# Even projection of a hybrid recurrent trunk: who asks for the channel-major tokens, and the order of the first pair of units

## What is computed

```python
p = jnp.einsum('bld,de->ble', rmsnorm(h, norm_w), w_in).astype(jnp.float32)
```

## Time and profile before

| what | value |
|---|---|
| median of three runs | 3124.69 us |
| lowest and highest run | 3123.67 and 3127.38 us |
| profiled execution, its own time | 3118.83 us |
| its span | 3117.0 us |
| TensorE (PE) matmul busy | 3001.8 us, 96% |
| PEld / VectorE (DVE) / ScalarE (ACT) / GpSimd (POOL) busy | 87% / 62% / 32% / 16% |
| mean DMA rate over the span | 100 GB/s |

### The profile page before, as it was taken

How to read it: one execution, slowest core, us unless ns; L and a number is a source line. 1 busy time by engine, 2 the same in 40 slices (tenths; PEclk the granted TensorE clock), 3 DMA queues, 4 the chain that set the end, 5 groups by cost and what they waited for, 6 DMA issues and landing times. The chain is left out here.

```text
span 3117.0 us, 89481 instructions
## 1 busy us (share of the span) xinstructions
PE 3001.8 (96%) x38740; PEld 2724.3 (87%) x38740; DVE 1931.6 (62%) x4060; ACT 1001.3 (32%) x2220; POOL 503.9 (16%) x519
## 2 busy tenths in 40 slices
PE   8899999997999999999989999999997999999998
PEld 8899999996888888888779999999995787888886
DVE  4312334445777777777545156776765787888886
ACT  4311210003333443343157122222223344444441
POOL 0000000001333433343310000000001111111112
PEclk9999999998999999999899999999998999999999
DMA  6521212215233333433353221221214223333333
GB/s 219 151 80 66 74 61 76 70 49 167 86 95 119 120 102 119 124 123 101 110 194 115 70 70 63 76 77 60 76 50 156 83 84 90 97 97 97 97 104 129
DMA packets 227704, 311.70 MB, mean 100 GB/s; under 512 B 34792, under 2 KB 166128, under 8 KB 227184
## 3 DMA queue, kind: packets, MB, share of 16 engines
q1 hardware_dynamic: 218160, 276.03, 27.7%
q0 software_dynamic: 9152, 29.94, 3.2%
HBM read 210.18 MB, written 95.72 MB: 98 GB/s over the span
## 5 line engine op out<-in xcount | busy, mean ns | idle before, releaser
L410 DVE SCALAR_TENSOR_TENSOR po_stage<-po_work,po_cw,po_stage 128x424 f32<-128x424 f32 (+1 forms) x360 | 232.1, 645 | 28.3 <-issue 1.7
L588 PE MATMUL po_ps<-po_xnT_hi,po_w_hi 128*128 128x424 f32 x960 | 205.0, 355 | 0.0
L588 PE MATMUL po_ps<-po_xnT_hi,po_w_lo 128*128 128x424 f32 x960 | 204.4, 355 | 0.0
L588 PE MATMUL po_ps<-po_xnT_lo,po_w_hi 128*128 128x424 f32 x960 | 204.1, 354 | 0.0
L302 ACT ACTIVATE po_work<-po_ps 128x424 f32<-128x424 f32 (+1 forms) x120 | 61.6, 514 | 408.1 <-PE po_ps L588 408.1
L588 PEld LDWEIGHTS po_ps<-po_xnT_hi,po_w_hi 128*128 128x128 f32 x960 | 180.3, 188 | 5.2
L588 PEld LDWEIGHTS po_ps<-po_xnT_hi,po_w_lo 128*128 128x128 f32 x960 | 180.4, 188 | 4.5
L588 PEld LDWEIGHTS po_ps<-po_xnT_lo,po_w_hi 128*128 128x128 f32 x960 | 180.2, 188 | 4.6
L588 PE MATMUL pe_ps<-pe_w_hi,pe_xnT_hi 128*128 128x256 f32 x1088 | 154.4, 285 | 19.3 <-ACT pe_xnT_hi L302 15.4
L588 PEld LDWEIGHTS pe_ps<-pe_w_hi,pe_xnT_hi 128*128 128x128 f32 x1088 | 140.7, 193 | 21.5 <-issue 17.3
L588 PE MATMUL pe_ps<-pe_w_lo,pe_xnT_hi 128*128 128x256 f32 x1088 | 153.5, 284 | 0.0
(11 more groups left out here) (463 smaller groups left out, 7138.6 us busy)
## 6 DMA issues: line engine op xcount, KB each, us to landing
me_ring<-scratch_w_lo SPq DMA_DIRECT2D x68, 512.0 KB, 3.8
mo_c<-scratch_ch_o SPq DMA_DIRECT2D x51, 512.0 KB, 3.6
scratch_ch_o<-po_stage SPq DMA_DIRECT2D x96, 212.0 KB, 1.9
scratch_tok_e<-pe_stage SPq DMA_DIRECT2D x136, 128.0 KB, 1.9
pe_raw<-in_w_in_e POOLq DMA_DIRECT2D x52, 256.0 KB, 4.2
me_xs<-scratch_ch_e SPq DMA_DIRECT2D x17, 768.0 KB, 6.4
po_raw<-in_w_in_o POOLq DMA_DIRECT2D x48, 256.0 KB, 3.8
scratch_ch_e<-pe_stage SPq DMA_DIRECT2D x52, 212.0 KB, 1.9
```

The source lines that it names most:

```text
L410: return nc.vector.scalar_tensor_tensor(out=o, in0=a, scalar=s, in1=b, op0=op0, op1=op1)
L588: last = nc.tensor.matmul(out, left.bitcast(F32R), right.bitcast(F32R), start=(i == 0 and k == 0), stop=(i == 2 and k == KD - 1))
```

## The change

Four things, all in the even projection:

- `products()`: in the first pair the second unit lags by two tiles. The list is now (0, 0), (0, 1), (0, 2), (1, 0), (0, 3), (1, 1), ... (0, 16), (1, 14), (1, 15), (1, 16).
- The requests for tile t+2, channel-major and token-major, move from SyncE's queue to ScalarE's: the first stands ahead of the rounding of tile t+1, the second behind the root of tile t. In the prologue the channel-major tile 1 is asked for ahead of both token-major tiles.
- ScalarE takes the root of tile t behind the rounding of tile t+1 (before: of t+1), and rounds unit 1's weights behind the first root.
- VectorE takes the rest of tile t+1, then the reciprocal of tile t (before: of t+1), then scales tile t+2; unit 1's weights are split behind the first reciprocal, ahead of the scaling of tile 2.

```diff
@@ def products()
-            for t in range(NT):
+            lag = 2 if late else 0
+            for t in range(NT + lag):
                 for u in range(EARLY):
-                    yield u, ("tok", t)
+                    if 0 <= t - u * lag < NT:
+                        yield u, ("tok", t - u * lag)
@@ @block.sync
+            if late:
+                load_xt(1)
             for t in range(0 if late else 1, XB):
                 load_x(t)
-                if late and t:
-                    load_xt(t)
...
-                if u == 0 and what[1] + XB < NT:
-                    if late:
-                        sp.wait_ge(s_xs, what[1] + 1)
-                        load_xt(what[1] + XB)
-                        sp.wait_ge(s_rt, what[1] + 1)
-                    else:
-                        sp.wait_ge(s_tr, what[1] + 1)
+                if u == 0 and what[1] + XB < NT and not late:
+                    sp.wait_ge(s_tr, what[1] + 1)
                     load_x(what[1] + XB)
@@ @block.scalar
             if late:
                 round_x(0)
                 round_weights(0)
-                root(0)
...
-            round_weights(1)
+                round_weights(1)
             for n, (u, what) in ORDER:
+                if late and u == 0 and what[1] + XB < NT:
+                    act.wait_ge(s_xs, what[1] + 1)
+                    act.dma_start(xT[what[1] % XB], x_in[:, what[1] + XB]).then_inc(s_xt[what[1] % XB], 16)
                 if u == 0 and what[1] + 1 < NT:
                     round_x(what[1] + 1)
-                    if late:
-                        root(what[1] + 1)
-                    elif what[1] + 2 < NT:
+                    if not late and what[1] + 2 < NT:
                         root(what[1] + 2)
+                if late and u == 0:
+                    root(what[1])
+                    if what[1] + XB < NT:
+                        act.wait_ge(s_rt, what[1] + 1)
+                        act.dma_start(x_sb[what[1] % XB], x[(what[1] + XB) * P:(what[1] + XB + 1) * P, :]).then_inc(s_x[what[1] % XB], 16)
+                    if what[1] == 0:
+                        round_weights(1)
@@ @block.vector
                 scale_x(1)
-                take_rstd(0)
...
-            split_weights(1)
+                split_weights(1)
             for n, (u, what) in ORDER:
                 if u == 0 and what[1] + 1 < NT:
                     split_x(what[1] + 1)
-                    if what[1] + 2 < NT:
+                    if what[1] + 2 < NT and not late:
                         scale_x(what[1] + 2)
-                    if late:
-                        take_rstd(what[1] + 1)
+                if late and u == 0:
+                    take_rstd(what[1])
+                    if what[1] == 0:
+                        split_weights(1)
+                if late and u == 0 and what[1] + 2 < NT:
+                    scale_x(what[1] + 2)
```

## The result

The changed kernel took 3098.33 us, the median of four runs (3103.8, 3094.2, 3097.84, 3098.82), beside 3124.18 us of the kernel before (3117.24 to 3127.38). The ratio is 0.9921, with a 95% interval of 0.9898 to 0.9944, so it is faster, by less than 1%.

| program | median, us | lowest to highest | ratio to before | interval |
|---|---|---|---|---|
| before (30 runs) | 3121.12 | 3108.87 to 3134.03 | | |
| before, as one of the variants | 3115.35 | 3107.28 to 3133.16 | 0.9994 | 0.9975 to 1.0013 |
| changed kernel | 3107.66 | 3088.80 to 3110.79 | 0.9949 | 0.9929 to 0.9968 |

A forecast was written before the change was run, and what follows sets the result against it. PE's pace, with waits for tiles held by the request-to-store circle, bounds the first pair: 5.8 + 17.8 = 23.6 us lost before, 7.2 after, gain 16.4, so 3124.7 - 16.4 = 3108.3 us, range 3103 to 3117.

The forecast's parts named there:

- The circle and its end, 17.8 us: First pair's middle tiles: request, transfer, scaling, read-out, store, next request take 7.11 us against 5.76; moving requests regains 17.8 us.
- The rule that the prediction weighed against the change: Requests on several engines save only issue time: 15 x 0.43 = 6.5 us less, 3118.2 us; as a rival, 4%.
- The start, 7.2 us: First products: 1.2 us idle before (0, 1), 4.4 before (0, 2), 1.6 of lower clock; 5.8 us lost before.
- about 114: Sign of being right: the first product of unit 2 starts at about 114 us, 130.71 before.
- that rival: Slower: ScalarE becomes the bound, requests reaching 5.76 us per tile at 1.4 us each; 3135 us at 2.3; 3%.
- The transfers: Middle tiles: a transfer takes 4.5 us, the DMA share rises from 0.57 to about 0.68; the circle bears 6.8 us.
- the second rival: Transfers become the bound in the middle tiles: at 8 us each, 9 us of the gain are lost, 3117 us; 8%.
- Given back later: Rival: PE's waits of later phases grow by what came early; time stays within 3119 to 3129 us; 3%.
- the prediction's 3102.4: Whole kernel: forecast in the profiled execution's own terms, which took 3118.83 us before, less the gain of 16.4 us.
- 2 us of spread: Whole kernel: allowance of 2 us that, with no lower clock at the start (1.6 us), sets the low end, 3105.
- costed the new places of root and reciprocal at nothing: Even projection: no matmul waits for root or reciprocal, only read-outs, which may be four products late; 0 us.

The follow-up runs named there:

- one store earlier: Kernel before, requests still on SyncE's queue in the old order but placed ahead of the store of (1, t) instead of behind it; 3093.66 us in one run.
- only the queue: Kernel before with nothing but the two requests moved to ScalarE's queue, no lag, old order of root, reciprocal and scaling; 3109.2 us in one run.
- the extra load: Changed kernel with a third, unused load of 512 KB per tile on ScalarE's queue ahead of the channel-major one; 3100.4 us in one run.
- the requests back on SyncE's queue: Changed kernel with the two requests back on SyncE's queue, lag and new order on ScalarE and VectorE kept; 3111.73 us over twelve runs, ratio 0.9968.
- before again: Kernel before, unedited, run again under another name to measure the spread; median 3115.35 us, ratio 0.9994.
- after again: Changed kernel, unedited, timed once more; median 3107.66 us, ratio 0.9949.
- only the queue, timed: Kernel before with only the two requests moved to ScalarE's queue, run again for its time; 3100.25 us over six runs, ratio 0.9935.

## Why the prediction was right and wrong

**The circle and its end, 17.8 us: right.** No wait of the middle is left, products stand 2.88 us apart, and "one store earlier" shows that the place behind the store's wait was the cause. The tile from which the prediction read the circle is a short one, 7.11 us; over the fourteen requests of the middle the mean is 7.38. The rule that the prediction weighed against the change (the Trainium skill, DMA: Bandwidth & Descriptors, Issuing engines are not separate DMA queues: only the sequencer's time is saved) would have meant 3118.2 us, at the price that the rows give for a request. The runs show 20.3 us less from the queue alone and 18.2 us, in unit 2's start, from a move on the same queue. The transfer itself was no shorter (a median of 4.7 us from request to landing both before and after), so for that the runs agree with it; what the change took away is a wait at the queue's head.

**The start, 7.2 us: 8.0 measured.** 1.5 us ahead of (0, 1) against 1.2; 4.3 us ahead of (0, 2) against 4.4; 2.1 us of low clock against 1.6 (1.6 in the repeat). Unit 2 came at 115.01 for "about 114", and the gain at that point is 15.7 us for 16.4.

**ScalarE: right.** A request takes 0.33 to 0.46 us for the 0.45 taken. Single ones in other kernels took up to 1.10 us ("only the queue"), still below the 1.4 at which that rival began. **The transfers: right.** 4.7 us for 4.5, share 0.69 for 0.68, and the extra load shows about from where on the second rival would have held. The reason given for the 4.5, that the other 512 KB are no longer asked for 0.5 us behind, has no support: see "the requests back on SyncE's queue".

**Given back later: open, for some 4 of the 15.7 us.** The projection ends 15.7 us earlier (709.2 for 724.9), but the odd projection starts only 10.2 us earlier (1583.2 for 1593.4), and 11.2 in the pair of repeats (1584.8 for 1596.0), because the even mixing between them took longer in both traces of the changed kernel. Other kernels whose projection ends as early (the one that fills the hole with the identity, and "one store earlier") don't show it: their even mixing took 869.0 and 870.2 us. That the spans differ by 15.2 us is in part luck: the odd mixing, which varies by 11 us in one program, happened to be 4.5 us shorter. The same luck brought the profiled execution, 3103.80 us, within 1.4 us of the prediction's 3102.4.

**What failed is the term "2 us of spread" in the range.** The forecast was set against the median of three runs that agree within 3.7 us, and the term was set below even those 3.7 us. Thirty runs of the same program lie between 3108.87 and 3134.03 (a single one in another set took 3143.01), and its profiled executions, with spans of 3110.0 and 3117.0, differ by 7.0 us while their even projections agree within 0.3 us. Medians of 12 and of 30 such runs lay 5.8 us apart; by estimate from these, a median of four runs against a median of three can be off by 5 to 10 us with every step of the sum right. A spread of 10 us in place of 2 would have given a range that holds both medians of the changed kernel, 3098.33 and 3107.66; the 10 is chosen after the fact. Where the first measurement shows 24.7 us, 16 is what the mechanism gives up to unit 2. That the other 9 are this spread is the likely reading, since the two intervals overlap from 17.5 to 22.2 us, but it is argued and not shown: the chip of the first measurement is not on record and may be another than that of the repeat, and no run explains the single executions of 3088.80 and 3092.00.

**What the prediction didn't see.** It costed the new places of root and reciprocal at nothing. True for this kernel, but only because the queue had already broken the circle: without the new queue the same move gives 14.1 us. The change holds two cures for one illness, and the better of the two alone (the queue, 3100.25 us, unit 2 at 110.62) beats the whole in the trace by 4.4 us. In time the two can't be told apart: their intervals overlap.

## What to carry to other kernels

Where a request for the next input stands behind a store on one in-order queue, look for a circle: if that store waits for a read-out that stands behind the same input, the whole round trip sets the pace, and the request belongs on another queue or one store earlier. Test each part of a compound change alone: two of these cured the same wait and the third cost up to 4 us. And compare phases of traces before whole times: here the phase resolved 0.4 us where single times lie more than 10 us to either side.

## What the hardware did that was not expected

**Where the spread lies.** Spans of the phases in us, from the starts of their matmuls (to the last matmul of the even projection, then to the odd projection's first, through the odd projection, to the end):

| execution | even projection | even mixing | odd projection | odd mixing | span |
|---|---|---|---|---|---|
| before | 724.9 | 868.5 | 768.0 | 755.6 | 3117.0 |
| before again | 724.6 | 871.4 | 769.5 | 744.5 | 3110.0 |
| after | 709.2 | 874.0 | 767.5 | 751.1 | 3101.8 |
| after again | 709.6 | 875.2 | 767.9 | 755.9 | 3108.6 |
| only the queue, timed | 704.8 | 872.5 | 767.3 | 752.4 | 3097.0 |

The even projection repeats within 0.4 us, the odd one within 2; the odd mixing phase varies by 11 us in the same program. The even mixing takes 868.5 and 871.4 us before, 874.0 and 875.2 in the changed kernel; over all fourteen traces it lies between 868.5 and 875.2. What varies in either mixing phase was not settled.

**The clock behind a hole.** At the start, a hole of 2.31 to 2.81 us was followed by a product of 2.97 to 3.42 us, and one of 3.58 to 5.02 us by a product of 4.31 to 5.29 us, instead of 2.88 (the 3.42 includes a wait of 0.21 us for the rest of tile 2). There a shorter hole is worth more than its own length: from 3.93 to 2.81 us it gave 1.1 us, and 1.5 us more behind it. The length of the hole alone doesn't decide it, though. In the middle of the kernel before, holes of up to 1.73 us were followed by products of 2.93 to 2.95 us, but in its repeat one of 2.05 us, behind earlier ones of 0.66 and 1.07, was followed by a product of 4.46 us, with a granted clock of 0.84 from 60 to 70 us:

```profile
66.68 2.03 PE L588 MATMUL pe_ps<-pe_w_hi,pe_xnT_hi 128*128 128x256 f32 x8 [2.05 <-ACT pe_xnT_hi L302]
...
71.14 1.12 PE L588 MATMUL pe_ps<-pe_w_hi,pe_xnT_hi 128*128 128x256 f32 x8
```

So the waits of the middle can cost the clock too, in some executions.

**Requests beside compute.** ScalarE's request at 43.29 runs while its read-out of 43.26 is still busy: this request took no compute time from it that the trace shows.
